# First quarters of the in-projection: eight of 24 blocks issued behind the scaling of the next quarter, and three weight splits issued earlier

## The reference, cut to what matters

```python
sc = jax.nn.silu(c); scc = jax.nn.silu(c_ctx)
shift_l, scale_l, gate_l = jnp.split((sc @ mod_w[l] + mod_b[l])[:, None, :], 3, axis=-1)
shift_c, scale_c, gate_c = jnp.split(scc @ mod_w[l] + mod_b[l], 3, axis=-1)
hl = xl * (1.0 + scale_l) + shift_l
hc = xc * (1.0 + scale_c) + shift_c
...
al, rl, kl, vl, wdl, adl, gl = split_even(hl @ w_in)
ac, rc, kc, vc, wdc, adc, gc = split_even(hc @ w_in)
```

## Time and profile before

| | before |
|---|---|
| median of 3 runs | 3786.3 us |
| lowest and highest run | 3783.22 and 3786.93 us |
| span of the profiled execution | 3776.6 us |
| TensorE busy | 3522.4 us (93%) |
| VectorE, ScalarE busy | 2039.3 us (54%), 1541.7 us (41%) |
| read from memory | 535.86 MB |

### The profile page before, as it was taken

One profiled execution on the slowest core, in us unless ns is written; L12 is line 12 of the kernel. 1 busy time (PEld: TensorE's weight loads), 2 busy tenths in 40 slices (PEclk: granted clock), 3 DMA queues, 4 the chain that ended last, 5 costly groups with the idle time before them and its releaser, 6 DMA issues. The chain is left out here.

```text
span 3776.6 us, 70993 instructions
## 1 busy us (share of the span) xinstructions
PE 3522.4 (93%) x31292; PEld 2922.0 (77%) x31292; DVE 2039.3 (54%) x3564; ACT 1541.7 (41%) x2599; POOL 247.0 (7%) x295
## 2 busy tenths in 40 slices
PE   6798999999999989899999899989999999999998
PEld 3576777777767767777887788658998899999887
DVE  1354465456444666764656465655444555555444
ACT  2343343344333433455543443435333444444433
POOL 0001111111011130011100000010000000000000
PEclk9999999999999999999999799899999999999999
DMA  9433343334323245433335444334553555555554
GB/s 378 157 115 102 105 121 108 95 118 124 102 85 103 71 152 192 156 123 101 101 114 178 156 150 134 106 106 158 188 169 132 167 180 181 182 182 180 190 185 161
DMA packets 349473, 548.57 MB, mean 145 GB/s; under 512 B 11724, under 2 KB 119916, under 8 KB 346988
## 3 DMA queue, kind: packets, MB, share of 16 engines
q1 hardware_dynamic: 346716, 538.78, 43.8%
q10 hardware_dynamic: 2448, 5.24, 0.4%
HBM read 535.86 MB, written 8.13 MB: 144 GB/s over the span
## 5 line engine op out<-in xcount | busy, mean ns | idle before, releaser
L301 PE MATMUL lane<-r,r 128*128 128x256 f32 (+1 forms) x8520 | 1506.4, 326 | 53.0 <-DVE r L259 43.0
L301 PE MATMUL bank<-r,r 128*128 128x512 f32 (+2 forms) x6360 | 1399.6, 359 | 61.5 <-DVE r L259 25.3
L301 PEld LDWEIGHTS lane<-r,r 128*128 128x128 f32 x8520 | 1279.2, 193 | 209.8 <-DVE r L259 48.0
L259 DVE TENSOR_TENSOR r<-ring,r 128x1024 fp32r<-128x1024 f32 x770 | 939.7, 1227 | 808.9 <-ACT r L298 807.5
L301 PEld LDWEIGHTS bank<-r,r 128*128 128x128 f32 x6360 | 1052.2, 195 | 262.7 <-ACT arena L298 30.6
L298 ACT ACTIVATE r<-ring 128x1024 fp32r<-128x1024 f32 x770 | 808.7, 1055 | 769.1 <-PE lane L301 572.3
L301 PE MATMUL lane<-arena 64*64 64x64 f32 (+4 forms) x12940 | 618.5, 252 | 44.6 <-issue 12.7
L301 PEld LDWEIGHTS lane<-arena 64*64 64x64 f32 (+3 forms) x12940 | 465.0, 138 | 208.4 <-issue 121.9
L298 ACT ACTIVATE arena<-lane 128x256 f32<-128x256 f32 (+3 forms) x578 | 249.1, 451 | 577.5 <-PE lane L301 453.5
L270 DVE COPY arena<-lane 128x256 f32<-128x256 f32 (+3 forms) x366 | 131.9, 361 | 281.4 <-PE lane L301 256.1
L259 DVE TENSOR_TENSOR arena<-arena 128x256 f32<-128x256 f32 (+7 forms) x568 | 260.1, 489 | 35.7 <-ACT arena L298 14.1
(11 more groups left out here) (94 smaller groups left out, 1233.6 us busy)
## 6 DMA issues: line engine op xcount, KB each, us to landing
ring<-in_w_gate_up SPq DMA_DIRECT2D x88, 1024.0 KB, 5.0
ring<-in_mod_w SPq DMA_DIRECT2D x73, 1024.0 KB, 5.2
ring<-in_ev_w_in SPq DMA_DIRECT2D x44, 1024.0 KB, 8.3
ring<-in_w_down SPq DMA_DIRECT2D x44, 1024.0 KB, 5.0
ring<-in_od_w_in SPq DMA_DIRECT2D x40, 1024.0 KB, 5.0
ring<-in_w_in SPq DMA_DIRECT2D x40, 1024.0 KB, 5.1
ring<-in_w_xkv SPq DMA_DIRECT2D x32, 1024.0 KB, 5.3
ring<-in_ev_w_out SPq DMA_DIRECT2D x28, 1024.0 KB, 5.2
```

The source lines that it names most:

```text
L259: return Nothing() if self.e is None else self.e.tensor_tensor(o, a, b, op)
L301: return Nothing() if self.e is None else self.e.matmul(o, l, r, start=start, stop=stop)
```

## The change

The scaling step `h0(q)` moves ahead of the `drain(now)` that writes out what is left of the quarter's product, and each piece of the modulation is followed by two blocks instead of three. So 16 of 24 blocks stay interleaved in passes 1 to 3, and eight stand behind `h0(q)` in the list. The helpers that make the later products are moved up in the file, and their lists `halves` and `split_` are now shared, so that inside the product of quarter 3, at the third and the seventh block of its last unit, `split_next()` can issue the load and the split of the first two units of head pair 1.

```diff
+    halves, split_ = [], []
...
+    def split_next():
+        if not halves:
+            more()
+        if halves:
+            hp, sm, pc, h = halves.pop(0)
+            split_.append((hp, blocks(pc, 1024 * h, h == 1, [(sm, 8 * h + k) for k in range(8)])))
+            if not halves:
+                more()
...
-        for u in us:
-            yield from ev_blocks(u, first_turn)
+        for i, u in enumerate(us):
+            for j, end in enumerate(ev_blocks(u, first_turn)):
+                if q == 3 and i == 2 and j in (2, 6):
+                    split_next()
+                yield end
...
             if k0 == KT - 4:
                 step("mod_row", 0, g, b)
             next(now, None)
-            next(now, None)
             if k0 == KT - 4:
                 step("mod_col", 0, g, bank(first_mod))
+        step("h0", q)
         drain(now)
-        step("h0", q)
```

More of the change, by code:

```diff
@@ L782, in bigs_of, with load_mod, modulations, more @@
             + [Sum(EV_G + 1024 + P * hp, "gate_in", hp)]
+    made, combined, lora_banks = [0], [-1], {}
+    ring_ev, ring_mod = Turn([0, 1]), Turn([2])
+    mod_todo = [(l, g, k0) for l, g in [(0, g) for g in range(8, 12)] + [(1, g) for g in range(12)] for k0 in range(0, KT, 4)]
+    mod_pieces = []
+    def load_mod():
+        if mod_todo and not mod_pieces:
+            l, g, k0 = mod_todo.pop(0)
+            mod_pieces.append((l, g, k0, piece("mod_w", l, k0, 4, g * 512, 512, ring_mod)))
+    def modulations():
+        while mod_todo or mod_pieces:
+            load_mod()
+            l, g, k0, pc = mod_pieces.pop(0)
+            if k0 == 0:
+                b = bank(mod_turn)
+            step("mod", l, g, pc, k0, b)
+            if k0 == KT - 4:
+                step("mod_row", l, g, b)
+            yield
+            if k0 == KT - 4:
+                step("mod_col", l, g, bank(mod_turn))
+                yield
+    big_sums = [(hp, sm) for hp in range(1, HPS) for sm in bigs_of(hp)]
+    spills = [Sum(P * (i // 2) + (EV_G if i % 2 else 0), "spill_out", i) for i in range(16)]
+    halves, split_ = [], []
+    def more():
+        if big_sums and combined[0] >= big_sums[0][0] - 2:
+            hp, sm = big_sums.pop(0)
+        elif spills:
+            hp, sm = None, spills.pop(0)
+        else:
+            return
+        pc = loaded(ring_ev, 0, KT, [sm])
+        for h in range(2):
+            halves.append((hp, sm, pc, h))
+    def split_next():
[6 more added lines that the diff above has]
+                more()
+    def products():
+        while True:
+            if len(split_) < 2:
+                split_next()
+            if not split_:
+                if not big_sums:
+                    return
+                yield False
+                continue
+            hp, u = split_.pop(0)
+            for j, end in enumerate(ev_blocks(u, ev_turn)):
+                if end and hp is not None and u.blocks[0][0].args[1:] == (2,):
+                    made[0] = hp
+                if j == 2:
+                    split_next()
+                    load_mod()
+                yield j == len(u.blocks) - 1
     step("start")
@@ L864, in unit @@
         yield "read_out"
[L867 to L933, removed]
```

## The result

The changed kernel takes 3750.77 us in the median (3747.76 to 3752.16, four runs), the kernel before 3784.76 us (3779.49 to 3786.93, four runs); the ratio is 0.991, with a 95% interval of 0.9896 to 0.9924. The forecast was 3758 us, with a range of 3752 to 3768.

What follows compares the result with a forecast made beforehand. TensorE, 93% busy, was taken as the bound, idling behind scaling chains and weight splits, with transfers level. Gains of 20.0, 1.9 and 6.4 sum to 28.3 us, and 3786.3 less that gives 3758.0 us, range 3752 to 3768.

Steps and rivals of the forecast that it cites:

- The failing step: Whole kernel: runs' median lies 9.7 us above the profiled span, so 3786.3 less 28.3 gives 3758.0 us.
- Order and chain: Passes 1 to 3: 24 matmuls moved behind the transpose bring it 5.44 us earlier each; scaling to next product stays 8.13 us.
- The sum of 28.3: First 177 us: 20.0 by quarter 3's product, 1.9 of low clock in it, 6.4 at the recurrence's first unit.
- Low clock: TensorE's reduced clock behind idle gaps disappears: 1.4 us in pass 2, 2.4 in pass 3, 1.9 in quarter 3's product.
- The term for the wait ahead of quarter 3: Before quarter 3's product 1.9 us stay idle without lowering the clock, so 1.9 us are gained; other end 0.
- Transfers: Passes 2 and 3: pieces land every 2.59 us against TensorE's pitch of 2.58, lead 0.6 to 2 us, cost nothing.
- The first unit: Recurrence's first unit: two of three splits done early, so `kk_sum` starts 4.75 us after `lora` instead of 11.17; 6.4 gained.
- Given back: Rival: a later wait for VectorE grows by the 6.4 us gained at the recurrence's start; 3764 us, chance 0.08.
- Gap not filled: Rival: moved matmuls in passes 1 to 3 wait for something the scaling chain makes; about 3780 us, chance 0.04.
- clock low in the passes: Rival: waits between pieces keep TensorE at 1.2 GHz in three passes; about +14, 3800 us, chance 0.02.
- The transfers bind: Rival: pieces take 2.85 us instead of 2.59 in two passes, losing up to 4 us; 3762 to 3765, chance 0.12.
- The fourth rival: Passes at 1.2 GHz: +37 us, less 16.7 of filled gaps and 6.4 of the unit; 3800 us, chance 0.02.

Runs made afterwards that it cites:

- e3_splits_only: The kernel before with only the early weight splits in quarter 3's product, passes and scaling as before: median 3777.04 us, ratio 0.9981 to the kernel before.
- e0_after_again: The changed kernel, nothing altered, timed again beside the kernel before: median 3748.29 us, ratio 0.9915.
- e9_after_more_transfers: The changed kernel with quarters 2 and 3 of x loaded a second time, 1 MiB each: median 3760.29 us, ratio 0.9942 to the kernel before.
- e2_quarters_only: The changed kernel without the two early split calls, eight blocks still behind the scaling: median 3757.92 us, ratio 0.9938 to the kernel before.
- e6_gap_filled_with_spare_work: The kernel before with 24 unread matmuls behind the scaling in each of passes 1 to 3: median 3779.08 us, ratio 0.9987.
- e10_after_third: The changed kernel, nothing altered, timed a third time beside the kernel before: median 3754.17 us, ratio 0.9926.

## Why the prediction was wrong

- **The failing step** is the one that ties the sum to a time: "the runs' median lies 9.7 us above the span, so 3786.3 - 28.3 = 3758.0". What lies around the span is 1.8 us (1.75 to 1.88) in every run. The other 7.9 us were the distance between the profiled execution, 3778.4 us, and a median of three runs that stood 4.7 us above the mean of 68. From the profiled execution's own time the same sum gives 3776.6 - 28.3 + 1.8 = 3750.1 (measured 3750.77, and 3751.5 in the mean); from the mean of before, 3753.3. That the first comes within 0.7 us of the median is luck: single executions of the changed kernel range from 3743.4 to 3759.5. The ends of the range, 3752 and 3768, hung on the same step. Three runs of before (3783.2 to 3786.9) could not show that its runs range over 17 us, from 3771 to 3788, and the prediction gave the level no width of its own.
- **Order and chain.** Transposes forecast at 63.0, 91.1 and 119.5 came at 62.5, 90.7 and 118.9; products at 71.1, 99.3 and 127.6 came at 70.6, 98.8 and 127.05. The chain stayed at 8.1 us. Right. The sum of 28.3 was 28.8 in the trace, and 30.1 with 2.4 either way in the runs.
- **Low clock.** It is gone at both quarters and at the unit, as forecast. The term for the wait ahead of quarter 3 ("so I take this 1.9 as gained") was right in two of three profiles of the changed kernel, and the third shows its other end. Its size was a little high: 18.25 - 16.61 = 1.6 us.
- **Low clock, sized from one execution.** 1.4 and 2.4 us behind the gaps are what one profile had; a second of before had it longer behind the first gap. The experiment with spare work puts all of it at 4.9 us in the runs and at 5.5 and 7.1 against the two profiles, where the prediction has 5.7.
- **Transfers.** That they and TensorE are level, "with the least cover of all", was right. That they cost nothing was not quite: TensorE waited 0.9, 3.5 and 0 us for pieces in three profiles, and in the second this made the chain 1.3 us longer. The lead of "0.6 to 2 us" was 0.3 by the prediction's own figures for the last piece of pass 3 (116.6 against 116.9). The window of the kernel after shows 409 GB/s. The Trainium skill (DMA: Bandwidth & Descriptors, "Where 436 GB/s comes from") says that the side of the memory, at about 358 GB/s, binds loads; this trace does not agree.
- **The first unit.** 4.60 us from `lora` to `kk_sum` against 4.75 forecast; 7.2 us in the runs (3.4 to 11.0) against 6.4. Right.
- **The rivals.** Given back: no, `e3_splits_only` keeps it. Gap not filled, clock low in the passes: neither happened. The transfers bind: clearly only with more taken from the pass, or more transfers put in. The fourth rival's "16.7 of filled gaps" is 16.3 from three times 5.44; nothing hangs on it.

## What to carry to other kernels

When a chain on two engines makes TensorE idle at the end of each round, look for work of the round that the chain does not need, and issue it behind the chain's start; it pays twice, by the time itself and by the clock that does not fall. Count how many blocks the chain can hide (here 8.1 us, less what else stands there, is some nine blocks of 0.68 us); more than that gained nothing here, and four left gaps of 3.4 us and more that still cost the whole low clock. Then look at what was hidden by the slack that is gone. Here it is the transfers: two more were free before and cost about 5 us now. And set a sum made on a trace against that execution's own time, not against the median of other runs, and give the range the scatter of single executions.

## What the runs showed of the hardware that was not expected

- How long TensorE's clock stays at its lower level (1.2 GHz) behind the same gap differs between executions of one program: 0.72 and 0.57 over the same 12 us, in two profiles of before. Behind 2.07 us of idle time ahead of quarter 3's product it fell in two of six profiles (72 matmuls in 18.23 and 18.25 us, `e0_after_again` and `e9_after_more_transfers`) and not in four (16.6 us: after, `e2_quarters_only`, `e6_gap_filled_with_spare_work`, `e10_after_third`).
- Idle times of 3.4 and 3.8 us cost as much low clock (nine matmuls in 3.74 and 4.21 us) as 6.5 us did (3.67 and 4.21 us); of 1.1 us none (2.34 us).
- Runs of one kernel on one chip range over 13 us in one session (3775.2 to 3788.3) with the mean clock between 0.965 and 0.970, while the time outside the span stays at 1.8 us. Over the 64 listed runs of before, 0.001 less of mean granted clock goes with 2.1 us more of time. The work behind `kk_sum`, which the variants share, takes 3597.8 to 3607.1 us in the thirteen profiles (before and its variants 3599.7 to 3607.0, the changed kernel and its variants 3597.8 to 3607.1); where in it the scatter arises, and why, is open.
